# Seven block products for eight in the up half of the second feed-forward

## The reference, cut to what matters

```
def rms_norm(x, gain):
    y = xf * lax.rsqrt(jnp.mean(xf * xf, axis=-1, keepdims=True) + EPS)
    return (y * gain.astype(jnp.float32)).astype(x.dtype)
...
def sq_relu_mlp(h, w1, w2):
    return jnp.square(jax.nn.relu(h @ w1)) @ w2
...
        h = h + sq_relu_mlp(rms_norm(h, mlp_norm_gain[layer]), mlp_w1[layer], mlp_w2[layer])
    return rms_norm(h, final_norm_gain)[:, N_META:]
```

## Time and profile before

| | us |
|---|---|
| median of 3 runs | 2773.19 (2771.89 to 2775.13) |
| the profiled execution | 2769.4 |
| its span | 2767.6 |
| PE busy | 2692.9 |
| DVE busy | 1328.1 |
| POOL busy | 925.8 |
| ACT busy | 752.3 |

### The profile page before, as it was taken

How to read it: one execution, slowest core, us unless ns; L and a number is a source line. 1 busy time by engine, 2 the same in 40 slices (tenths; PEclk the granted TensorE clock), 3 DMA queues, 4 the chain that set the end, 5 groups by cost and what they waited for, 6 DMA issues and landing times.

```text
span 2767.6 us, 43631 instructions
## 1 busy us (share of the span) xinstructions
PE 2692.9 (97%) x18459; PEld 2423.2 (88%) x18459; DVE 1328.1 (48%) x1552; ACT 752.3 (27%) x1177; POOL 925.8 (33%) x403
## 2 busy tenths in 40 slices
PE   7998999999999999999999999999989999999998
PEld 7897998999999999999888888887768888888887
DVE  5387887442222322235677777779353222222234
ACT  3116886120100010002344344444221000110003
POOL 3130001344433443344323232324334444444441
PEclk9999999999999999999999999999999999999999
DMA  4110000111111111113111111112111111111111
GB/s 158 31 31 8 0 0 15 47 39 46 46 47 47 48 45 46 53 46 107 33 39 32 39 32 39 32 38 91 42 33 52 46 46 46 52 45 45 46 52 70
DMA packets 178141, 125.49 MB, mean 45 GB/s; under 512 B 4818, under 2 KB 171044, under 8 KB 177990
## 3 DMA queue, kind: packets, MB, share of 16 engines
q1 hardware_dynamic: 176694, 118.47, 14.0%
q10 hardware_dynamic: 1296, 4.73, 0.4%
HBM read 114.80 MB, written 8.39 MB: 45 GB/s over the span
## 4 chain that ended last, share of the span: by engine, by line
PE 84%; DVE 9%; issue 4%; ACT 3%; DMA 0%; ACTq 0%; SPq 0%; DVEq 0%
PE ps L1337 74%; PE ps L1471 3%; PE ps L1596 2%; PE ps L1564 1%; DVE kk L1172 1%; ACT prob L618 1%; PE ps L1421 1%; PE ps L1634 1%; ACT kk L716 1%; DVE kk L1169 1%; DVE tmp L901 1%; DVE y L967 0%; PE ps L1609 0%; DVE ssq L893 0%; DVE amax L1008 0%
## 5 line engine op out<-in xcount | busy, mean ns | idle before, releaser
L1337 PE MATMUL ps<-xh,wsp 128*128 128x512 f32 (+2 forms) x4864 | 1122.5, 355 | 13.8 <-POOL wsp L497 6.3
L495 POOL TENSOR_TENSOR wsp<-raw,ones 128x1024 fp32r<-128x1024 f32 x198 | 383.5, 1937 | 1784.8 <-PE ps L1337 1749.7
L1337 PEld LDWEIGHTS ps<-xh,wsp 128*128 128x128 f32 x4864 | 840.5, 189 | 100.3 <-issue 15.3
L1337 PE MATMUL ps<-xl,wsp 128*128 128x348 f32 (+2 forms) x2432 | 617.7, 351 | 0.0
L1337 PE MATMUL ps<-ah,wsp 128*128 128x348 f32 (+2 forms) x2560 | 567.0, 350 | 0.0
L497 POOL TENSOR_TENSOR wsp<-raw,wsp 128x1024 fp32r<-128x1024 f32 x198 | 533.5, 2694 | 15.5
L1337 PEld LDWEIGHTS ps<-ah,wsp 128*128 128x128 f32 x2560 | 443.1, 188 | 44.7
L1337 PEld LDWEIGHTS ps<-xl,wsp 128*128 128x128 f32 x2432 | 430.9, 189 | 44.3
L666 ACT ACTIVATE tmp<-tmp 128x1044 f32<-128x1044 f32 (+1 forms) x64 | 68.5, 1071 | 1096.1 <-DVE tmp L1070 555.6
L1337 PE MATMUL ps<-al,wsp 128*128 128x348 f32 (+1 forms) x1280 | 322.5, 349 | 0.0
L1337 PEld LDWEIGHTS ps<-al,wsp 128*128 128x128 f32 x1280 | 225.2, 188 | 23.2
(11 more groups left out here) (212 smaller groups left out, 2688.0 us busy)
## 6 DMA issues: line engine op xcount, KB each, us to landing
raw<-in_w SPq DMA_DIRECT2D x128, 512.0 KB, 3.7
raw<-in_c_w_in SPq DMA_DIRECT2D x40, 512.0 KB, 3.8
raw<-in_ab_w_in SPq DMA_DIRECT2D x12, 512.0 KB, 3.7
xst<-in_x SPq DMA_DIRECT2D x8, 512.0 KB, 6.6
raw<-in_ab_w_out SPq DMA_DIRECT2D x8, 512.0 KB, 3.5
h_kept<-h ACTq DMA_DIRECT2D x8, 512.0 KB, 2.6
h<-h_kept SPq DMA_DIRECT2D x8, 512.0 KB, 5.8
out<-ost SPq DMA_DIRECT2D x16, 256.0 KB, 3.0
```

What stands on the lines that cost most here:

```text
L495: nc.gpsimd.tensor_tensor(wsp[:, slot, 0, :], raw[:, slot, :], one, ALU.mult).then_inc(w_high, 1)
L1337: ins = M(ps[:, 3 * s + c, 0:n], w(a, k), b(k)[:, c0:c0 + n], start=(k == first and a == 0 and b is xa), stop=(k == last and a == 1))
```

## The change

The up half is one product of a 4096 x 1024 matrix (the weights, turned) by a 1024 x 1024 one (the tokens). It is cut into 16 pairs of hidden tiles. For a pair, weights and tokens are each cut into four blocks: the weights by tile (0, 1) and by half of the width, the tokens by half of the width and by 512 columns. A 2 x 2 block product of this kind needs eight block products; a Winograd form makes it with seven, of sums of blocks. Each of the seven is 4 x 3 = 12 matmuls of 512 columns. The changed kernel runs all 16 pairs first and then all eight down chunks.

- The sums of token blocks (`t2`, `t3`, `t4`, `x12`, `ts`) are made once, by DVE and ACT, after the projection.
- The sums of weight blocks are made by POOL for each pair (four subtractions or additions of 128x512), and POOL splits all seven operands (`high`, `low`) into four slots `wop`.
- ACT copies the first product out of PSUM, DVE combines the rest into the four quarters `hid`, applies relu and factor, ACT squares, and the tiles are stored to memory (`hidden_rows`) and loaded again, in the down half, into the two rows of `tmp`, where ACT rounds and DVE subtracts (`hidden_high`, `hidden_low`).

```
+            def high(g, a):
+                if g < 2:
+                    pool.wait_ge(w_used, U_MLP1 - 1)
+                elif g < 4:
+                    pool.wait_ge(z_ready, HG_LAST + KT)
+                else:
+                    pool.wait_ge(t_done, g - 3)
+                nc.gpsimd.tensor_tensor(operand(g, 0), a, one4, ALU.mult).then_inc(t_high, 1)
+
+            def low(g, a):
+                pool.wait_ge(t_high, g + 1)
+                nc.gpsimd.tensor_tensor(operand(g, 1), a, operand(g, 0), ALU.subtract).then_inc(t_low, 1)
...
+            add(sw0, sw1[:], weight(0, 0), ALU.subtract)
+            pool.wait_ge(t_add, 2)
+            pool.wait_ge(n_ssq, 21)
+            add(sw2, sw0[:], weight(1, 0), ALU.subtract)
...
+            def down_split(i):
+                if i < 2:
+                    pool.wait_ge(t_done, 7 * PAIRS - (1 if i == 0 else 0))
+                split(U_MLP1 + i, i % 2, 8 * (U_MLP1 + i - i % 2) + 16)
```

SP's queue at the turn from up to down:

```
+            def hidden_load(t):
+                if t == 0:
+                    sp.wait_ge(n_rc, 12)
+                elif t == 1:
+                    sp.wait_ge(t_low, 7 * PAIRS)
+                else:
+                    sp.wait_ge(l_l, 32 + t - 1)
+                for half in range(2):
+                    sp.wait_ge(s_hid[2 * (t % 2) + half], 16 * (t // 2 + 1))
+                nc.sync.sem_inc(c_sp, 1)
+                nc.sync.dma_start(tmp[:, t % 2, N_META:TOK], hidden_rows[t]).then_inc(s_re[t % 2], 16)
+
+            hidden_load(0)
+            down_load(0)
+            down_load(1)
+            hidden_load(1)
+            for t in range(2, CH):
+                hidden_load(t)
+            for i in range(2, 32):
+                down_load(i)
+                if i + 2 < 32:
+                    hidden_load(i + 2)
```

ACT: the stores, and what it does ahead of the last pair's squares:

```
+            def keep(p, n, b):
+
+                act.wait_ge(t_sq, 4 * p + n + 1)
+                nc.scalar.dma_start(hidden_rows[2 * p + b // 2][:, (b % 2) * HALF_T:(b % 2 + 1) * HALF_T], hid[b][:]).then_inc(s_hid[b], 16)
...
+                if p == PAIRS - 1:
+                    act.wait_ge(t_done, LAST + 2)
+                    for t in range(CH):
+                        hidden_high(t)
```

DVE: the token sums ahead of the first pair's quarters, and the down half:

```
+            def sum_third(i):
+                V.scalar_tensor_tensor(t3s[:, i, :], quarter(h, CH + i, 1), gain[:, CH + i:CH + i + 1], x12[:, i, :], ALU.mult, ALU.subtract).then_inc(x_s, 1)
...
+            def relu_half(b):
+
+                half = rms[:, N_META + (b % 2) * HALF_T:N_META + (b % 2 + 1) * HALF_T]
+                V.scalar_tensor_tensor(hid[b][:], hid[b][:], 0.0, half, ALU.max, ALU.mult).then_inc(t_relu, 1)
...
+            def hidden_low(t):
+                dve.wait_ge(l_h, 32 + t + 1)
+                V.tensor_tensor(hl[t // CH % 2][:, t % CH, N_META:TOK], tmp[:, t % 2, N_META:TOK], hh[t // CH % 2][:, t % CH, N_META:TOK], ALU.subtract).then_inc(l_l, 1)
...
+            for c in range(8):
+                for k in range(KT):
+                    add(E_MLP1 + 8 * c + k, k % 2, k, True)
+                    if c == 7:
+                        finish(4, k, False)
+                    elif k % 2:
+                        hidden_low(4 * (c + 1) + k // 2)
```

PE: a product, the order of the first pair, and the down half:

```
+            def product(p, s, high, low, ready=None):
+
+                g = 7 * p + s
...
+                pe.wait_ge(t_low, g + 1)
+                for k in range(CH):
+                    if ready is not None:
+                        ready(k)
+                    for side, x in ((0, high), (0, low), (1, high)):
+                        ins = M(product_bank(p, s), wop[:, g % 4, side, k * P:(k + 1) * P], x(k),
+                                start=(k == 0 and side == 0 and x is high), stop=(k == CH - 1 and side == 1))
+                ins.then_inc(t_done, 1)
...
+            product(0, 4, *s2, part_ready(13, 1))
+            product(0, 5, *s3, part_ready(17, 1))
+            product(0, 6, *s4, part_ready(21, 1))
...
+            pe.wait_ge(t_rd, 6 * PAIRS)
+            for c in range(8):
+                down(U_MLP1 + 4 * c, E_MLP1 + 8 * c, 32 + 4 * c, hh[c % 2], hl[c % 2], REAL)
...
             def down(u, e, l, high, low, cols):
 
                 pe.wait_ge(l_l, l + CH)
```

More of the change, by code:

```diff
@@ L509, in _, with landed, add @@
             split(U_HG + 41, 1, 8 * (U_HG + 40) + 16)
-            with pool.Fori((U_HG + 42) // 2, (U_MLP1 + 64) // 2) as i:
+            with pool.Fori((U_HG + 42) // 2, (U_HG + 50) // 2) as i:
+                for slot in range(2):
+                    split(i * 2 + slot, slot, i * 16 + 16)
+            one4 = ones[:, 0:1].rearrange("p (a b) -> p a b", b=1).to_broadcast([P, CH, P])
+            def landed(p, part):
+                pool.wait_ge(t_land[part], 16 * (p + 1))
+            def add(a, left, right, op):
+                nc.gpsimd.tensor_tensor(a[:], left, right, op).then_inc(t_add, 1)
@@ new lines, in _ @@
+            landed(0, 0)
+            high(0, weight(0, 0))
+            low(0, weight(0, 0))
+            landed(0, 1)
+            add(sw1, weight(0, 1), weight(1, 1), ALU.add)
+            pool.wait_ge(t_add, 1)
+            high(1, sw1[:])
+            low(1, sw1[:])
+            high(2, weight(1, 0))
+            low(2, weight(1, 0))
+            add(sw0, sw1[:], weight(0, 0), ALU.subtract)
+            pool.wait_ge(t_add, 2)
+            pool.wait_ge(n_ssq, 21)
+            add(sw2, sw0[:], weight(1, 0), ALU.subtract)
@@ new lines, in _, with hidden_high @@
+            sum_high(6, t2h[:, 2, :], ts[:, 2, :])
+            sum_high(7, t2h[:, 3, :], ts[:, 3, :])
+            for i in range(CH):
+                sum_high(8 + i, t3h[:, i, :], t3s[:, i, :])
+            for i in range(CH):
+                sum_high(12 + i, t4h[:, i, :], ts[:, i, :])
+            norm_root(3)
+            copy_first(1)
+            norm_copy(3)
+            def hidden_high(t):
+                act.wait_ge(s_re[t % 2], 16 * (t // 2 + 1))
+                A(hh[t // CH % 2][:, t % CH, real], tmp[:, t % 2, real], ACT.Copy).then_inc(l_h, 1)
@@ L831, in _ @@
+            square(PAIRS - 1, 2, 3)
+            keep(PAIRS - 1, 1, 2)
+            square(PAIRS - 1, 3, 1)
+            keep(PAIRS - 1, 2, 3)
+            keep(PAIRS - 1, 3, 1)
+            for b in range(4):
+                act.wait_ge(s_hid[b], 16 * PAIRS)
+            for t in range(CH, 32):
+                if t >= 2 * CH:
+                    act.wait_ge(z_ready, E_MLP1 + 8 * (t // CH - 1))
+                hidden_high(t)
             for k in range(KT):
-                finish(3, k)
-            norm(3)
@@ L1523, in up, with down @@
                         norm_sum(n)
-            def down(u, e, l, c0, cols):
+            def down(u, e, l, high, low, cols):
                 pe.wait_ge(l_l, l + CH)
@@ new lines, in _ @@
+            product(0, 6, *s4, part_ready(21, 1))
+            for p in range(1, PAIRS):
+                product(p, 0, *b11)
+                product(p, 1, *s2)
+                if p == 1:
+                    norm_bcast(3)
+                if p == 2:
+                    pe.wait_ge(n_rc, 12)
+                product(p, 2, *b21)
+                product(p, 3, *s4)
+                product(p, 4, *d12)
+                product(p, 5, *s3)
+                product(p, 6, *b22)
+            pe.wait_ge(t_rd, 6 * PAIRS)
```

331 lines of the change are left out of this document (318 added, 13 removed).

## The result

The changed kernel takes **2835.2 us** (median of 4 runs, 2833.33 to 2836.26) against 2772.54 us (2768.07 to 2775.13) for the kernel before, run beside it on the same chip. The ratio is 1.0227, with an interval from 1.0213 to 1.0241: 63 us slower. The prediction was 2852 (2812 to 2895) and slower at 0.96. The profiled execution took 2835.8 us and its span is 2833.8, 66.2 above the span before.

The account below looks back on a forecast made before the run. PE bounds the kernel before, POOL the changed up half. Down start 2449.5 + 356.2 products + 18.5 between chunks + 1.7 clock = 2826, +79 us; on 2769.4 that is 2848.6, plus 3.8 to the median: 2852 (2812 to 2895).

Parts of the forecast that it names:

- The bound moves to POOL: Up half: a pair takes POOL 24.5 us against PE's 19.5, so POOL sets the pace.
- Two signs: Up half profile: every product of PE waits for L635, after some 0.7 us idle; PE's share near 80%.
- A POOL instruction of 512 columns: Up half: 1.05 us for a high, 1.30 for a low or sum, with an assumed constant of 0.2.
- the first rival: Up half: POOL is cheaper; halved durations alone 28.8 us less, 2823; no turn costs either, 2793; chance 0.12.
- The pair: Up half: POOL's instructions, gaps and turns with DVE's relus make 24.5 us a pair.
- 18 x 0.07 us of gaps: Up half, each pair: a gap of 0.07 us for every one of POOL's eighteen instructions.
- The first pair: Start of up half: POOL waits 14.7, 7.8 and 5.0 us, 3 us more unrecovered; product 6 ends at 2076.5.
- The turn: From up to down: hidden tiles 1 and 3 reload in sequence; down half starts 13.5 us after the last low.
- Between chunks: Down half: DVE's eighth addition and fourth subtraction stand uncovered, 2.65 us seven times, 18.5 us.
- The clock: At the turn: PE's 10.5 us idle brings one fall to 1.2 GHz, costing 1.7 us.
- the fourth rival: Up half: PE loses its clock in the gaps; four pairs at that level make 58 us, 2910; chance 0.05.
- The sum: End of the down half: 2826 against 2746.7 now, +79 us.

Follow-up runs that it names:

- boundary: Changed kernel with DVE's last subtraction of a down chunk one addition earlier, after the seventh output tile: 2811.78 us, 1.0148 times before.
- best kernel: all3 plus ACT making five more highs around the first pair, and DVE's scales and three bank reads between its token sums: 2754.17 us, 0.9937 times before.
- all3: Changed kernel with boundary, act_highs, and own memory for a pair's last sum so hidden tile 1 loads early: 2763.58 us, 0.9964 times before.
- short_relus: Changed kernel with DVE's relus covering 16 of 512 columns, so the output differs: 2818.3 us.
- act_highs: Changed kernel with ACT making four of the seven highs from pair 2 on: 2788.08 us, 1.0054 times before.

## Why the prediction was right, and where its sizes were off

**The bound moves to POOL.** Right, and shown both ways: with POOL's sums away the up half runs at PE's pace, and with four highs moved to ACT nearly so. Two signs that went with it were wrong. I had every product wait for L635 after some 0.7 us of idle, and PE's share near 80%. PE waits once a pair, some 2.2 us, before product 1, because the two dependent sums stand there and POOL gets ahead again elsewhere; and its share is 90%, part of it at the lower clock. The pace of a pair does not depend on how the idle is spread, so the time did not suffer.

**A POOL instruction of 512 columns.** Right within 0.01 us: 1.04, 1.29 and 1.30. The constant part, from 1.04 at 512 and 1.90 at 1024 columns, is 0.18 us. Halved durations alone, the first rival, would have been 18 x 0.09 = 1.6 us a pair too low.

The Trainium skill, GPSIMD Engine Reference, section 3.1 (elementwise cycle accounting), had led to an estimated constant of 0.30 us; the runs here have 1.29 and 2.40 us for 512 and 1024 columns of a subtraction, so 0.18, and the measurement decides.

**The pair.** The rate was over-estimated, 24.5 us for 23.35. The failed term is 18 x 0.07 us of gaps. Gaps stand behind the seven highs and behind the two sums whose result the next instruction reads; behind a low there is none, and the next instruction even starts 0.04 us before the recorded end. On balance that leaves 0.4 of the 1.26 us, so 0.9 of the miss is here, 0.1 in the durations and 0.1 in the turns: 0.38 us a relu for 0.4. Over the up half this moved the last low from the predicted 2436 to 2419.6, 16.4 us, the largest miss.

**The first pair.** Right in its path, and in its end partly by luck: product 6 ended near 2075.4, predicted 2076.5. POOL's waits were 11.6, 7.2 and 4.2 us for a predicted 14.7, 7.8 and 5.0, 4.5 less together. Against that its first high started at 2008.63 and not at 2006.5, and its first eight instructions lost 2.4 us in turns for which the prediction had nothing. The price on DVE's queue behind the sums was put at 3 us; POOL then waited 3.9.

**The turn.** 12.36 us from the last low to the down half for a predicted 13.5, by the very chain that was named. Tile 1's subtraction met no turn (1.24 us): POOL's split of the first down unit began at 2420.21 and was nearly over at 2424.50. PE idled 9.05 us for a predicted 10.5.

**Between chunks.** 2.43 us seven times, 17.0 for 18.5, at the place named; boundary takes it away.

**The clock.** One fall was counted, 1.7 us. In the down half the falls cost 1.9 us in the first chunk and 1.5 in each of two others, 4.9 in all. How many come is not fixed: four other kernels with this order had three behind the first chunk. In the first pair the clock was low for 20.5 us while PE waited for DVE. In the up half nine falls of 3.4 us came, the mechanism of the fourth rival, but each for a short time only: PE waits for POOL there and makes it good in its slack, and no pair is longer for it.

**The sum.** -16.4 at the last low, -1.15 at the turn, +4.6 in the down half (381.0 for 376.4: clock +3.2, idle -1.5, and eight separate pieces of 44.87 us for 356.2 in one, +2.8) make -13: +66 us for +79. The other 4 us between 2852 and 2835 are the distance of the median from the profiled execution, 3.8 us before and none here.

**Still open.** Some 15 us of PE idle remain in the first pair of the best kernel, while DVE makes the token sums. Running two pairs' products of plain blocks first would cover part of them; it was not tried. Why the clock falls where it does, after nine of 13 nearly equal idles in the up half and after two of seven between chunks, is not settled. Of the 5.3 us that all3 missed in the up half, some 4 may be the lows on which product 1 of a pair waits; no run tests that.

## What to carry to other kernels

Saving an eighth of a stage's matmuls is worth 44 us only if the engine that prepares operands keeps up: here a pair went from 8.6 us of preparation to 21.9, part of it the constant that each small instruction pays. Count the preparing engine's time for one unit of work against the saved engine's, before anything else, and give work to whichever engine idles (ACT here). Then look at the ends of the restructured stage: one subtraction a place too late in a queue cost 21 us, a third of the loss.

## What the runs showed of the hardware

- POOL's subtraction, 512 columns: 1.29 us, 1024 columns: 2.40; a product with ones: 1.04 and 1.90. Both have a constant of about 0.18 us.
- Behind an instruction whose result the next one needs POOL loses 0.08 us, behind another nothing.
- A DVE instruction with both inputs in SBUF and a POOL instruction take turns at 512 columns too: 0.38 us for POOL (0.87 at 1024), and up to 1.2 us for DVE, whose relu of 0.68 us takes up to 1.84. Against a POOL instruction of 1024 columns it took 2.88.
- The granted clock fell to half for 3.4 us nine times in the up half, each time within 4 us of the start of an idle of PE of 2.2 to 2.35 us. Four more idles of 2.0 to 2.35 us had no fall behind them, and of the seven of 2.43 us between chunks two had one. With no idle over 0.93 us in the same stretch (short_relus), and with none over 0.10 (act_highs, 2100 to 2340), it did not fall once. In the up half PE was not the bound, and the falls cost nothing.
